# Prompt attention of a hybrid decoder step: forming 1 - a on VectorE with a two-tensor subtraction for one head and on GpSimd for the other

## The reference

```
z = einsum('bqhd,bkhd->bhqk', q, k) * SB_HEAD_DIM ** -0.5 + bias
vis = k_pos[None, :] < q_pos[:, None]
log_keep = where(vis, log_sigmoid(-z), 0)
after = cumsum(log_keep, axis=3, reverse=True) - log_keep
a = where(vis, exp(log_sigmoid(z) + after), 0)
out = einsum('bhqk,bkhd->bqhd', a, v)
```

## Time and profile before

| | |
|---|---|
| median of 3 runs | 2906.96 us (2906.63 to 2909.41) |
| the profiled execution | 2908.15 us, of which the span of the instructions is 2906.3 us |
| granted TensorE clock, mean | 0.932 of full speed |
| busy share of the span | PE 86%, PEld 54%, DVE 49%, ACT 28%, POOL 35% |
| line 1561, the scan | 128 instructions, 473.0 us |
| line 1588, the weight products | 128 instructions, 398.8 us |
| line 1559, 1 - a | 128 instructions, 175.9 us |

### The profile page before, as it was taken

The page is one execution under the profiler, slowest core; times in us unless marked ns, Lnnn a source line. Parts: engine busy times, 40 slices in busy tenths (PEclk is TensorE's granted clock), DMA queues, the critical chain, the costliest instruction groups (busy, mean ns, idle before and its releaser), DMA issues. The chain is left out here.

```text
span 2906.3 us, 37872 instructions
## 1 busy us (share of the span) xinstructions
PE 2503.2 (86%) x14073; PEld 1568.7 (54%) x14073; DVE 1422.4 (49%) x1669; ACT 813.6 (28%) x1746; POOL 1021.5 (35%) x546
## 2 busy tenths in 40 slices
PE   5999899998599996999999667878888876886998
PEld 3555444443244443888888654555555554553443
DVE  1111066576100002555555319999999983442333
ACT  2222031223000001222222115656565642221110
POOL 2434010101000001435444005898898970002554
PEclk9999899999799997999999758999898998997999
DMA  5232212220522102011011121000000008994332
GB/s 155 90 96 92 47 30 45 61 60 15 93 64 70 59 31 65 27 39 43 29 43 33 46 99 64 30 30 1 30 30 1 30 1 291 330 325 164 127 127 83
DMA packets 150639, 224.91 MB, mean 77 GB/s; under 512 B 15632, under 2 KB 86241, under 8 KB 145416
## 3 DMA queue, kind: packets, MB, share of 16 engines
q1 hardware_dynamic: 150536, 223.50, 24.7%
HBM read 154.55 MB, written 68.91 MB: 77 GB/s over the span
## 5 line engine op out<-in xcount | busy, mean ns | idle before, releaser
L1561 DVE TENSOR_TENSOR_SCAN f_x<-f_x 128x2064 f32<-128x2064 f32 (+15 forms) x128 | 473.0, 3696 | 4.4
L1588 POOL TENSOR_TENSOR f_a<-f_a,f_x 128x2063 f32<-128x2063 f32 (+15 forms) x128 | 398.8, 3124 | 124.9 <-DVE f_x L1561 124.9
L629 PE MATMUL ps<-hT,wa 128*128 128x512 f32 (+1 forms) x960 | 354.4, 532 | 45.3 <-DMA wa<-w_in 45.3
L447 PE MATMUL ps<-hT,wc 128*128 128x512 f32 (+1 forms) x960 | 355.4, 532 | 12.8 <-DMA wc<-w_in 12.8
L629 PEld LDWEIGHTS ps<-hT,wa 128*128 128x128 f32 x960 | 168.7, 191 | 230.6 <-issue 185.1
L1456 PE MATMUL ps<-con,f_a 128*128 128x128 f32 x1216 | 189.7, 296 | 102.1 <-POOL f_a L1588 102.1
L447 PEld LDWEIGHTS ps<-hT,wc 128*128 128x128 f32 x960 | 169.1, 192 | 198.3 <-issue 198.3
L2010 PE MATMUL ps<-m_w,m_mT 128*128 128x512 f32 x544 | 238.1, 596 | 0.0
L321 PE MATMUL ps<-wt,hT_now 128*128 128x512 f32 x544 | 237.7, 595 | 0.0
L1511 ACT ACTIVATE f_at<-ps 128x512 f32<-128x512 f32 (+3 forms) x352 | 182.2, 539 | 197.6 <-PE ps L1456 195.2
L1456 PEld LDWEIGHTS ps<-con,f_a 128*128 128x128 f32 x1216 | 139.9, 149 | 138.7 <-POOL f_a L1588 108.7
(11 more groups left out here) (277 smaller groups left out, 3514.6 us busy)
## 6 DMA issues: line engine op xcount, KB each, us to landing
j_kp<-cache_k SPq DMA_DIRECT2D x128, 256.0 KB, 4.1
j_v<-cache_v SPq DMA_DIRECT2D x128, 256.0 KB, 4.7
chan<-y SPq DMA_DIRECT2D x12, 1088.0 KB, 6.0
chan<-ya SPq DMA_DIRECT2D x12, 1088.0 KB, 4.8
d_ld<-chan SPq DMA_DIRECT2D x16, 768.0 KB, 5.3
h_rows<-hg SPq DMA_DIRECT2D x17, 512.0 KB, 4.9
m_hh<-h_rows SPq DMA_DIRECT2D x17, 512.0 KB, 5.0
xin<-x_prompt SPq DMA_DIRECT2D x16, 512.0 KB, 4.1
```

Source lines behind the costliest of these rows:

```text
L447: m = pe.matmul(ps[:, ci, 0:n], wc[k][:, c, :], hT[:, c, c0:c0 + n], start=(c == 0), stop=(c == KC - 1))
L629: m = pe.matmul(ps[:, ci, 0:n], wc[k][h % 2][:, c, :], hT[:, c, c0:c0 + n], start=(c == 0), stop=(c == KC - 1))
L1561: dve.tensor_tensor_scan(dst[:, ::-1], dst[:, ::-1], dst[:, ::-1], 1.0, ALU.mult, ALU.bypass).then_inc(scanned, 1)
L1588: pool.tensor_tensor(w, w, x_at(u, h, i)[:, 1:], ALU.mult).then_inc(weighed, 1)
```

## The change

For the first head of a pair, VectorE forms 1 - a with a subtraction of two tensors: a column of ones, `f_one` (128 x 1, read again for every column), minus `f_a`. For the second head, GpSimd forms it with the multiplication by -1.0 and the addition of 1.0 that VectorE used before. The semaphore `kept` becomes one per head, and the scan of each head waits for its own. The 64 VectorE instructions of the second heads go; GpSimd gets 64 instructions, one in front of each pair of weight products, each with a wait for ScalarE's last chunk of that row. TensorE's first wait counts one more (the memset of the ones).

```
-    z_acc, z_read, kept, scanned, weighed = ... p.sem("kept") ...
+    kept = [p.sem("kept_first_head"), p.sem("kept_second_head")]
...
+        one = sb("one", P, 1)
...
         @block.vector
+            dve.memset(one[:, :], 1.0).then_inc(filled, 1)
...
-                        dve.wait_ge(z_read, START + 2 * n - 1 + h)
                         dst = x_at(u, h, i)
-                        dve.tensor_scalar(dst, a_at(u, h, i)[:, M0:], -1.0, 1.0, ALU.mult, ALU.add).then_inc(kept, 1)
-                        dve.wait_ge(kept, START + m + 1)
+                        if h == 0:
+                            if u >= 2 and i == 0:
+                                dve.wait_ge(weighed, START + 4 * (u - 1))
+                            dve.wait_ge(z_read, START + 2 * n - 1)
+                            dve.tensor_tensor(dst, one[:, 0:1].broadcast_to([P, row_width(r)]), a_at(u, h, i)[:, M0:], ALU.subtract).then_inc(kept[0], 1)
+                        dve.wait_ge(kept[h], START + m + 1)
                         dve.tensor_tensor_scan(dst[:, ::-1], dst[:, ::-1], dst[:, ::-1], 1.0, ALU.mult, ALU.bypass).then_inc(scanned, 1)
...
         @block.gpsimd
                     for i, r in enumerate(unit_rows[u % UNITS]):
+                        n += len(row_chunks(r))
+                        pool.wait_ge(z_read, START + 2 * n)
+                        pool.tensor_scalar(x_at(u, 1, i), a_at(u, 1, i)[:, M0:], -1.0, 1.0, ALU.mult, ALU.add).then_inc(kept[1], 1)
                         for h in range(2):
                             pool.wait_ge(scanned, START + 4 * u + 2 * i + h + 1)
```

More of the change, by code:

```diff
@@ L1370, in prompt_attention @@
     gate_loaded = p.sem("pgate_loaded")
-    z_acc, z_read, kept, scanned, weighed = p.sem("z_acc"), p.sem("z_read"), p.sem("kept"), p.sem("scanned"), p.sem("weighed")
+    z_acc, z_read, scanned, weighed = p.sem("z_acc"), p.sem("z_read"), p.sem("scanned"), p.sem("weighed")
+    kept = [p.sem("kept_first_head"), p.sem("kept_second_head")]
     turned, evacuated, av_done = p.sem("A_turned"), p.sem("AT_evacuated"), p.sem("av_done")
@@ L1469, in values @@
                 m.then_inc(av_done, 1)
-            pe.wait_ge(filled, START + 2)
+            pe.wait_ge(filled, START + 3)
             for s in range(NU + LAG):
@@ L1546, in _ @@
             dve.memset(v[:, 0, :], 0.0).then_inc(filled, 1)
+            dve.memset(one[:, :], 1.0).then_inc(filled, 1)
             dve.tensor_copy(eye[:, :], p.ident)
             dve.tensor_copy(hide[:, :], p.con[:, C_NM:C_NM + P]).then_inc(filled, 1)
+            dve.wait_ge(filled, START + 3)
             for u in range(NU):
@@ L1553, in _ @@
                     for h in range(2):
-                        m = 4 * u + 2 * i + h
-                        if u >= 2 and i == 0 and h == 0:
-                            dve.wait_ge(weighed, START + 4 * (u - 1))
-                        dve.wait_ge(z_read, START + 2 * n - 1 + h)
+                        m = 2 * u + i
                         dst = x_at(u, h, i)
-                        dve.tensor_scalar(dst, a_at(u, h, i)[:, M0:], -1.0, 1.0, ALU.mult, ALU.add).then_inc(kept, 1)
-                        dve.wait_ge(kept, START + m + 1)
+                        if h == 0:
[4 more added lines that the diff above has]
+                        dve.wait_ge(kept[h], START + m + 1)
                         dve.tensor_tensor_scan(dst[:, ::-1], dst[:, ::-1], dst[:, ::-1], 1.0, ALU.mult, ALU.bypass).then_inc(scanned, 1)
@@ L1583, in _ @@
                 if u < NU:
+                    n = chunk0[u]
                     for i, r in enumerate(unit_rows[u % UNITS]):
+                        n += len(row_chunks(r))
+                        pool.wait_ge(z_read, START + 2 * n)
+                        pool.tensor_scalar(x_at(u, 1, i), a_at(u, 1, i)[:, M0:], -1.0, 1.0, ALU.mult, ALU.add).then_inc(kept[1], 1)
                         for h in range(2):
```

## The result

The changed kernel takes 2982.99 us (median of 4 runs, 2978.98 to 2983.72) against 2906.8 us before: 1.0258 times as long, 95% interval 1.024 to 1.0275, that is +76.2 us. Forecast were 2989 us, +82.

What follows compares the result with a forecast made beforehand. The prediction took VectorE and GpSimd to form a single queue in the stage. Its terms, -3 + 71.6 + 13 = +82 us, gave 2989 us by the median, with an 8 in 10 range of 2960 to 3052 us.

Steps and rivals of the forecast that it cites:

- Point 1: VectorE's own part: four TENSOR_SCALARs a unit replaced by two two-tensor subtractions over half the columns; -3 us, between -6 and 0.
- Point 2: VectorE's subtraction, with two SBUF inputs, still excludes GpSimd and so counts in the queue; no separate size.
- Point 3: GpSimd's 64 new TENSOR_SCALARs over 70,656 columns, priced like its COPY at 1.013 ns a column: 71.6 us, none beside other work.
- Rival A: GpSimd's TENSOR_SCALAR is as slow as its two-tensor products: +142 us, 3049 us; chance 0.31, with TensorE becoming the bound included.
- Point 4: New order: GpSimd's instructions follow each other, exposing start-ups while VectorE waits before the second scan; +13 us, between 0 and 26.
- Rival B: VectorE's subtraction stays out of the queue, its column of ones being no second stream: -8 us, 2899 us; chance 0.05.
- Rival C: GpSimd's one-input TENSOR_SCALAR runs beside VectorE's scans, so its 71.6 us fall out: +3 to +10, some 2912 us; chance 0.04.
- Rival D: TensorE becomes the bound because more waiting lowers its clock below 0.67; no chance of its own, folded into the upper end.

Runs made afterwards that it cites:

- The subtraction alone: Against the kernel before: first head subtracted on VectorE as in the changed kernel, second head keeps VectorE's TENSOR_SCALAR, GpSimd gets nothing new; 2945.18 us, 1.0132.
- ScalarE version: Kernel before, with 1 - a of the second head formed by ScalarE as sigmoid(-z) from the scores, not by VectorE; 2865.08 us, 0.9854.
- control of the two banks: The changed kernel with two PSUM banks in place of three for the transposed weights and nothing else new; 2983.09 us.
- GpSimd's part alone: Against the kernel before: second head's 1 - a on GpSimd as in the changed kernel, first head by VectorE's TENSOR_SCALAR; 2944.15 us, 1.0124.

## Why the prediction was right

**What bounds the stage.** The step on which all rests, that VectorE and GpSimd form one queue in this stage, held. It was read from durations that did not fit their widths and from one unit's sum, against a busy share that pointed to VectorE. The scan that reads its second input from PSUM shows it: 159 us of "busy" scan time vanish, and the whole is 154 us shorter. That the two are so close is chance, since TensorE sets the new time. One reading of the prediction was short: the 5.02 us of the two gate products are not the scan's alone, which ends at 1808.40; the TENSOR_SCALAR of 1808.33 then holds the second of them until 1809.55, by the same queue.

**Point 1, VectorE's own part, -3 us.** The subtraction alone measures the exchange of one head, +37.6 us. The work of the other head, taken out of VectorE by the ScalarE version, is worth -42.0. Together -4.4 us, inside the -6 to 0 stated; but each of the two is known to some 5 us only, so this can't tell the -3 that I took from 0 or from -6. The price was right too: 1.88 us for 1680 columns, 1.119 ns a column, for the 1.115 assumed.

**Point 2, the subtraction excludes GpSimd.** Shown by moving its ones to PSUM, -67 us, with the control of the two banks at 0.

**Point 3, GpSimd's TENSOR_SCALAR, 71.6 us.** Two arithmetic steps cost no more than a copy. The rows that nothing holds (four each) give 1587 ns for 1680 columns and 1161 for 1168:

```profile
L1593 POOL TENSOR_SCALAR f_x<-f_a 128x1680 f32<-128x1680 f32 x4 | 6.3, 1587 | 0.0
...
L1593 POOL TENSOR_SCALAR f_x<-f_a 128x1168 f32<-128x1168 f32 x4 | 4.6, 1161 | 0.0
```

That is 426/512 = 0.83 ns a column and a start-up of 0.19 us; two of them in a unit of 2208 columns take 2.22 us, 71 us in all. Rival A, 1.5 ns or more, fell by this row. The line rate that the Trainium skill states (GPSIMD Engine Reference, Engine selection) for one-input work fits: the 58.9 us that the prediction estimated from it are 0.83 ns a column. The 1.8 cycles a column that the prediction took from the page's section Elementwise — side-by-side cycle accounting are not the price of this instruction.

**Point 4, the order, +13 us.** This is the term that seems too large. GpSimd's part alone cost +36.6 over before, and without the second head VectorE is worth -42.0: the rest is 78.6 us, of which the TENSOR_SCALARs are 71 and about 8 are left for start-ups in the open. (The -42.0 carries the ScalarE version's own side effects, and each of the two times is known to some 5 us, so the 8 is rough; it lies within the 0 to 26 stated.) The three start-ups are there as described (gate product, gate product, TENSOR_SCALAR, product, each right behind the other), but the scan now begins 0.06 us after the product and has its own start-up covered. That is my reading of the timeline; no run measured it apart. The forecast was 6 us too high for about this reason.

**Rival B's price.** Its condition, a subtraction outside the queue, is what the ones in PSUM made, and the time was 2916 us and not the 2899 that I gave it. I had let all of GpSimd's new work lie beside the subtraction. The rows of that run show a TENSOR_SCALAR that comes 0.30 us behind a scan and is held through it, with VectorE's second scan waiting for it; over the stage, 93.5 us of VectorE's idle time were ended by GpSimd's TENSOR_SCALARs (82.2 in the changed kernel). So even under B the change would not have gained.

**Rival C** fell by the TENSOR_SCALAR of 4.57 us under a scan. **Rival D** did not come: TensorE's granted clock went from 0.89 to 0.88 in the middle of the stage, and its wait for GpSimd from 102.1 to 144.0 us; busy for 123.68 of 160 us, it was not the bound of the changed kernel.

## What to carry to other kernels

If an instruction's duration does not fit its width, look at what runs on the other engine at its start and its end: VectorE at 99% was here one of two engines in a single queue. In such a queue, moving work from one member to the other gained nothing here, and it lost by what the work cost more there; only work that leaves both (to ScalarE, 42 us) or an instruction that stops excluding the other (an input moved to PSUM, 154 us) counts. And an operand that does not enter the result can still cost: the scan named its own buffer a second time, and that second reading was what held GpSimd.

## What the runs showed of the hardware that was not expected

- A column of ones broadcast from SBUF counts as a full second input: in the changed kernel the subtraction takes 3873 ns at most, held by a product of GpSimd, against 2307 with the column in PSUM.
- A broadcast input from PSUM costs VectorE next to nothing: 1276 ns in the mean of 64 subtractions, a mean of 1104 columns; the scan of 2064 columns takes 4.45 us, against 4.46 from SBUF.
- The kernel with the scan's input in PSUM, at 2753.36 us, is faster than both kernels by 5.3% of the one before and 7.7% of the changed one.
